# Another order of the three interleaved chains in a layer's mixer

## The chip, the cores and the metric

The kernel runs on one core of one Trainium2 chip. The metric is the device time of one execution in microseconds (us), lower is better. The engines are TensorE (PE, its weight loads shown as PEld), VectorE (DVE), ScalarE (ACT), GpSimd (POOL), and SyncE (SP), which here issues the transfers.

## The reference, cut to what matters

The network is a first block (window attention, a state space mixer, a delta rule mixer, a feed-forward part) and then two layers. The change touches only the mixer of the first of these layers, the "even mixer", on 512 tokens:

```python
h = x @ w_in                       # q_a, c_kv, q_idx, k_idx, w_idx, q_b, k_b, v_b, f_in
q_lat = einsum('bshd,hrd->bshr', q_a, w_uk) * HEAD_DIM ** -0.5
log_f = log_sigmoid(f_in + b_f); cum_f = cumsum(log_f, axis=1)
# for each block of 128 queries:
idx = einsum('bthd,bsd->bths', qi, k_idx)
score = einsum('bth,bths->bts', wi, relu(idx))      # masked to be causal
_, sel = top_k(score, k_sel)                        # 128 keys of each query
la = ql @ c_sel + bias[t5_bucket];  oa = softmax(la) @ c_sel      # 8 latent heads
lb = qb @ k_b + cum_f - cum_f_keys; ob = softmax(lb) @ v_b        # 8 forget heads
out = concat([oa @ w_uv, ob]) @ w_o
```

## The kernel before

All matrix products with large weights are made of three passes of float32r halves (helper `three`, L570 to L572): high by high, high by low, low by high. The weights come in a list of chunks; ACT makes the high half of a chunk (L1260), DVE or, for chunks 52 to 63, POOL the low half (L2450).

In the even mixer each engine runs the same three generators, and `walk` steps them in the order of one string of 444 letters, `even_order()`. A letter is a step of a chain, and each engine meets its own part of that step at this place of its in-order queue:

- **F** (156 steps), `dense_even`: the projection, chunks 53 to 62. A step is the three passes of one of 8 slices of k into a bank of 512 columns (chunk 56, the second half of the values, takes 12 products of 256 columns in a step). The last four steps turn the output of the forget heads (`otb`) for the output product.
- **I** (96 steps), `index`: three steps for small work (the decay sums among it), then for each of three query blocks 8 score steps (PE L1019 `ps<-kiT,qiT`, ACT relu into `rel` L1617, DVE sum into `sco` L2233) and 16 top-k steps on DVE alone; at last 8 heads of latent queries (`ql`, L1030) and position bias (`near`, L1036), with four steps for the values `va` (L1044).
- **A** (192 steps), `units`: 64 attention units, one for each head and query block, in three stages with lag: scores (L1054, L1058), turning the probabilities (L1076), and the product with the values (L1091, `ota` or `otb`).

All index products of PE go through one bank, number 7: the next one waits until ACT has emptied it. ACT's relu in turn waits until DVE has summed the relu two heads back, since `rel` has two buffers:

```python
clear(7)
w.wait_ge(*even.act.at("ki"))
e.matmul(ps[7][:, 0:n], qiT[...], kiT[s, 0:n], ...).then_inc(*idx.pe.one("s", i, h))
bank[7] = [idx.act.at("relu", i, h)]
```

`kiT` is what ACT copies out of the second bank of chunk 55 (L1575), and the product of chunk 55 with all its slices stands ahead of it. The engines' code of the stage stands in `dense_even`, `index` and `units` of each engine's program, called by `walk(EVEN_ORDER, ...)` at L1097, L1664, L2292, L2586 and L2720. The first and the odd mixer have orders of their own.

Of the kernel before, what the change touches and what calls it, by code (L numbers as in the profile page):

```python
# [246 lines left out]


def even_order():
    return ("FFFFFIFFFFFFFFFFFFFFFFFFFFFIFFFFFFFFFFFFFFFFIFFFFFFFIFIFFIFIFIFIFIFIFFFIFFIIFFIIIIFFFFIIFFFFIFIIFAFIFFFIIIFFIFFIAFAFFAIA"  # L250
            "AAAIAAFAIAAIAFAFIAIFFIAIFAAAAFFAAIAAFIAAIFAAIAAIAIFAIFAAAFAIFIFAIFFFFIIAAIAIAFFIAFAFAAIFFAAIAAIAFFAIFFIAFIAFAIAAFAFIAFAI"
            "AFAIAIIAAFAAIFIFFAIAAFFIAAAFFFFFAAFFIAIAAAFIAAFIAIFFIFAAIAAAFIIAAFAFIAFAAAAIAAIAFIAAIFAIAAFIAAAAAIAAAAAIAAAFAAAAIAAAAAFI"
            "AFAAFAIAAAAIAAAAAAAFAFIAAAAFAIAAAAAIAAAAIAAAAAAAAAAIAAAAAAAAAAIAAAAAAAFAAAAFAAAFAAFA")


def odd_order():
# [5 lines left out]
def build(nc, ins, out):  # L262
    plan = weight_plan()
    offs = [0]
    for c in plan:
        offs.append(offs[-1] + 128 * chunk_width(c))
    u_dram = nc.dram_tensor("u_scratch", (8, 384), F32, kind="Internal").ap()
    IN_ORDER, EVEN_ORDER, ODD_ORDER = first_order(), even_order(), odd_order()

    ctx = ExitStack()  # L270
# [2597 lines left out]
```

## Time and profile before

| | before |
|---|---|
| median of 3 runs | 1930.08 us (1929.76 to 1931.78) |
| profiled execution, its own time | 1931.88 us |
| span of the profiled execution | 1930.0 us |
| PE busy | 1877.8 us (97%) |
| DVE, ACT, POOL busy | 978.8, 731.5, 249.5 us |
| mean granted clock of TensorE | 0.987 |

The even mixer's walk takes from 721 to 964 us of the span. A row of a timeline gives the start in us from the start of the span, the duration, the engine, the source line, the operation, what it writes and reads, the count, and, in brackets, the idle time of the engine before it and what ended it. A matmul's duration overlaps the next one, so the pace of PE is read from the distance of two starts.

### The profile page before, as it was taken

To read this page: it belongs to the slowest core of one execution; us is meant where nothing else is said; L and a number is where in the kernel's file an instruction comes from. 1 tells how busy PE (TensorE), PEld (TensorE's weight loads), DVE (VectorE), ACT (ScalarE), POOL (GpSimd) and SP (SyncE) were. 2 spreads that over 40 slices of the span, in tenths; PEclk is the share of its full clock that TensorE was granted. 3 is DMA by queue.
4 is the path that set the end of the run, shared out by engine and by line. 5 is a ranking of instruction groups with operands and counts; after the bars stand their busy time and mean duration, and the time that the engine had idled before them with its cause. 6 is when DMAs were issued, how large, how long until landed. Compare 5 with 4: busy or idle time off the path is not lost.

```text
span 1930.0 us, 23339 instructions
## 1 busy us (share of the span) xinstructions
PE 1877.8 (97%) x9766; PEld 1548.4 (80%) x9766; DVE 978.8 (51%) x1557; ACT 731.5 (38%) x1229; POOL 249.5 (13%) x168
## 2 busy tenths in 40 slices
PE   7999978999999999999999999999999999999998
PEld 6888967888888888767789888888778888888886
DVE  5676455323222254776566555522664475555334
ACT  6664444323231243556724434421333244434211
POOL 1433500111110023211000111100000001111000
PEclk9999979999999999999999999999999999999999
DMA  5211022132323232101022232232322313222321
GB/s 197 87 37 64 29 89 88 66 109 88 109 88 109 76 132 95 66 23 45 14 78 103 92 108 89 94 135 76 109 88 87 110 66 109 92 105 87 120 98 66
DMA packets 28764, 170.01 MB, mean 88 GB/s; under 512 B 3386, under 2 KB 5602, under 8 KB 10866
## 3 DMA queue, kind: packets, MB, share of 16 engines
q1 hardware_dynamic: 28660, 168.53, 25.4%
q8 instruction: 77, 1.26, 0.3%
q14 instruction: 27, 0.22, 0.0%
HBM read 166.37 MB, written 2.11 MB: 87 GB/s over the span
## 4 chain that ended last, share of the span: by engine, by line
PE 90%; DVE 8%; ACT 1%; issue 1%; DMA 0%; POOL 0%; SPq 0%; DVEq 0%; ACTq 0%
PE ps L570 26%; PE ps L572 26%; PE ps L571 26%; PE ps L1091 2%; DVE wL L1781 1%; PE ps L1019 1%; PE ps L1054 1%; PE ps L1058 1%; PE ps L1076 1%; DVE x L2316 1%; DVE x L2311 1%; DVE hL L1788 1%; PE ps L685 1%; PE ps L650 1%; PE ps L849 0%
## 5 line engine op out<-in xcount | busy, mean ns | idle before, releaser
L570 PE MATMUL ps<-hH,wH 128*128 128x512 f32 (+1 forms) x1568 | 604.2, 385 | 7.8 <-DVE hL L1788 4.8
L571 PE MATMUL ps<-hL,wH 128*128 128x512 f32 (+1 forms) x1568 | 592.0, 378 | 0.0
L572 PE MATMUL ps<-hH,wL 128*128 128x512 f32 (+1 forms) x1568 | 592.0, 378 | 0.0
L1781 DVE TENSOR_TENSOR wL<-raw,wH 128x1024 fp32r<-128x1024 f32 (+2 forms) x250 | 306.2, 1265 | 378.2 <-ACT wH L1260 378.2
L1260 ACT ACTIVATE wH<-raw 128x1024 fp32r<-128x1024 f32 (+2 forms) x298 | 290.5, 1024 | 281.8 <-PE ps L572 281.8
L570 PEld LDWEIGHTS ps<-hH,wH 128*128 128x128 f32 x1568 | 297.2, 190 | 69.1 <-issue 5.9
L572 PEld LDWEIGHTS ps<-hH,wL 128*128 128x128 f32 x1568 | 296.8, 189 | 54.2
L571 PEld LDWEIGHTS ps<-hL,wH 128*128 128x128 f32 x1568 | 297.2, 190 | 52.6 <-issue 1.4
L570 PE MATMUL ps<-wH,aH 128*128 128x512 f32 x528 | 209.0, 396 | 0.0
L571 PE MATMUL ps<-wL,aH 128*128 128x512 f32 x528 | 208.8, 395 | 0.0
L572 PE MATMUL ps<-wH,aL 128*128 128x512 f32 x528 | 208.8, 395 | 0.0
L2336 DVE SCALAR_TENSOR_TENSOR ft<-ps,cols,ft 128x511 f32<-128x511 f32 (+1 forms) x176 | 131.4, 746 | 133.1 <-ACT ft L1689 130.0
L2450 POOL TENSOR_TENSOR wL<-raw,wH 128x1024 fp32r<-128x1024 f32 (+3 forms) x48 | 111.9, 2351 | 341.9 <-ACT wH L1260 341.9
L2549 POOL TENSOR_TENSOR aL<-ft,aH 128x512 fp32r<-128x512 f32 x44 | 57.1, 1297 | 683.7 <-ACT aH L1695 683.7
L570 PE MATMUL ps<-wH,hH 128*128 128x512 f32 (+2 forms) x320 | 115.6, 361 | 3.6 <-DVE wL L1781 3.6
L572 PEld LDWEIGHTS ps<-wH,aL 128*128 128x128 f32 x528 | 99.3, 188 | 24.0
L570 PEld LDWEIGHTS ps<-wH,aH 128*128 128x128 f32 x528 | 99.3, 188 | 23.8
L571 PEld LDWEIGHTS ps<-wL,aH 128*128 128x128 f32 x528 | 99.3, 188 | 23.8
L572 PE MATMUL ps<-wH,hL 128*128 128x512 f32 (+2 forms) x320 | 111.7, 349 | 0.0
L571 PE MATMUL ps<-wL,hH 128*128 128x512 f32 (+2 forms) x320 | 111.7, 349 | 0.0
L1689 ACT ACTIVATE ft<-ps,cols 128x512 f32<-128x512 f32 x88 | 59.9, 681 | 72.0 <-PE ps L572 72.0
L2160 DVE TENSOR_TENSOR ft<-ft,ps 128x512 f32<-128x512 f32 x22 | 15.1, 687 | 120.4 <-PE ps L572 120.4
(370 smaller groups left out, 1907.9 us busy)
## 6 DMA issues: line engine op xcount, KB each, us to landing
raw<-in_wbig SPq DMA_DIRECT2D x139, 1024.0 KB, 4.9
rows<-in_rows SPq DMA_DIRECT2D x12, 512.0 KB, 5.9
x<-in_x SPq DMA_DIRECT2D x8, 512.0 KB, 5.4
raw<-in_wbig SPq DMA_DIRECT2D x8, 512.0 KB, 3.5
out<-x SPq DMA_DIRECT2D x4, 512.0 KB, 2.6
near<-u_scratch SPq DMA_DIRECT2D x1, 1024.0 KB, 6.9
raw<-in_wbig SPq DMA_DIRECT2D x1, 1000.0 KB, 7.5
raw<-in_wbig SPq DMA_DIRECT2D x1, 600.0 KB, 10.2
```

The lines of the kernel that those rows point to most:

```text
L570: e.matmul(o, hi, m_hi, start=first, stop=False)
L571: e.matmul(o, hi, m_lo, start=False, stop=False)
L572: return e.matmul(o, lo, m_hi, start=False, stop=end)
L650: m = e.transpose(ps[b][:, 128 * k:128 * k + 128], src[:, o:o + 128], ident[:, :])
L685: m = e.matmul(ps[b][:, 128 * j:128 * j + 128], v3(da)[:, i, h:h + 1].broadcast_to([128, 128]), U[:, :], start=True, stop=True)
L1091: t = e.matmul(ps[6][:, 0:64], Pt[n % 2][:, 128 * j:128 * j + 128], v[:, j, 64 * h:64 * h + 64], start=j == 0, stop=j == i)
L1260: e.activation(wH[r][:, cs], raw[r][:, cs], ACT.Copy).then_inc(*cast.one(c, h))
L1689: e.activation(ft[s][:, :], ps[b0 + t][:, :], ACT.Identity, scale=cols[:, column + 2:column + 3]).then_inc(*ffn.act.one("y", c, t))
L1781: e.tensor_tensor(wL[r][:, cs], raw[r][:, cs], wH[r][:, cs].bitcast(F32), ALU.subtract).then_inc(*low_dve.one(c, h))
L2336: e.scalar_tensor_tensor(y[:, d:512], ps[b0 + t][:, 0:512 - d], cols[:, column + 2 - d:column + 3 - d], y[:, d:512], ALU.mult, ALU.add).th ...
L2450: e.tensor_tensor(wL[r][:, cs], raw[r][:, cs], wH[r][:, cs].bitcast(F32), ALU.subtract).then_inc(*low_pool.one(c, h))
L2549: e.tensor_tensor(aL[:, m, :], ft[t0 + m % 2][:, :], aH[:, m, :].bitcast(F32), ALU.subtract).then_inc(*ffn.pool.one("lo", c))
```

## The change

The string that `even_order()` returns is replaced by another with the same 156 F, 96 I and 192 A. Each chain keeps its own order; only how they are interleaved changes, on all five engines at once. Nothing else changes: same operations, tiles, banks and waits.

```diff
 def even_order():
-    return ("FFFFFIFFFFFFFFFFFFFFFFFFFFFIFFFFFFFFFFFFFFFFIFFFFFFFIFIFFIFIFIFIFIFIFFFIFFIIFFIIIIFFFFIIFFFFIFIIFAFIFFFIIIFFIFFIAFAFFAIA"
+    return ("FFFFFIFFFFFFFFFIFFFFIFFFFFFFFFFFFFFFFFFFFFFFFFFFFFFIFIFIIIIFIFIIFFFIIFFFFFIFIFFIIIFIIFIFFFFFFIFFFIAIFFIAIIFAIFFAIAFIAAAI"
...
-            "AFAAFAIAAAAIAAAAAAAFAFIAAAAFAIAAAAAIAAAAIAAAAAAAAAAIAAAAAAAAAAIAAAAAAAFAAAAFAAAFAAFA")
+            "FIAAAAAIAAAIAAAAAAAAIAAAIAAAAAAAAAIAAAIAAAAAAAAAAIAAAIAAAAAAAAFAAAAAAAAAAAAFAAAFAAFA")
```

Counted over the string, the maximal groups of F steps with another product of PE on each side are 61 before and 54 now. The last F step that is not one of the four turns is letter 388 before and letter 361 now, of 444; the first of the four turns is letter 431 before and 423 now.

**PE, the first index score.** `wH_51`, `wL_53` with `hH_56`, `hL_57` as the second operand are chunk 56 (256 columns), `hH_56<-wH_52` 512 columns wide is chunk 55, `kiT_181,qiT_177` is the first score product. Before:

```order
L572 MATMUL ps<-wH_51,hL_57 128x256
L570 MATMUL ps<-wH_51,hH_56 128x256
L571 MATMUL ps<-wL_53,hH_56 128x256
L572 MATMUL ps<-wH_51,hL_57 128x256
L1019 MATMUL ps<-kiT_181,qiT_177 128x256
```

Now:

```order
L570 MATMUL ps<-hH_56,wH_52 128x512
L571 MATMUL ps<-hL_57,wH_52 128x512
L572 MATMUL ps<-hH_56,wL_54 128x512
L1019 MATMUL ps<-kiT_181,qiT_177 128x256
L570 MATMUL ps<-wH_51,hH_56 128x256
```

The first step of chunk 56 (12 products) stood between chunk 55 and the score; now the score follows chunk 55 directly.

**PE, the third to the sixth score of the first query block.** Before, there was a step of chunk 56 (12 products) behind each of them, as here around the third:

```order
L571 MATMUL ps<-wL_53,hH_56 128x256
L572 MATMUL ps<-wH_51,hL_57 128x256
L1019 MATMUL ps<-kiT_181,qiT_178 128x256
L570 MATMUL ps<-wH_51,hH_56 128x256
L571 MATMUL ps<-wL_53,hH_56 128x256
```

Now:

```order
L572 MATMUL ps<-wH_51,hL_57 128x256
L1019 MATMUL ps<-kiT_181,qiT_178 128x256 x2
L1019 MATMUL ps<-kiT_181,qiT_179 128x256 x2
L570 MATMUL ps<-wH_51,hH_56 128x256
```

The four follow each other with nothing between them.

**ACT, from the copy of `kiT` on.** `wH_52<-raw_50` are the two casts of chunk 57, `rel` the relus of the scores, `vb` the copies out of the banks of chunk 56:

```order
 L1575 ACTIVATE ckvT_174<-ps 128x512
 L1575 ACTIVATE kiT_181<-ps 128x512
-L1260 ACTIVATE wH_52<-raw_50 128x1024 x2
 L1617 ACTIVATE rel_202<-ps 128x256
-L1560 ACTIVATE vb_188<-ps 128x256
+L1260 ACTIVATE wH_52<-raw_50 128x1024 x2
 L1617 ACTIVATE rel_203<-ps 128x256
 L1560 ACTIVATE vb_188<-ps 128x256
 L1617 ACTIVATE rel_202<-ps 128x256
 L1617 ACTIVATE rel_203<-ps 128x256
-L1560 ACTIVATE vb_188<-ps 128x256
 L1617 ACTIVATE rel_202<-ps 128x256
```

The first relu now stands ahead of the two casts, the second directly behind them. On SP the two transfers of the decay sums (L2713, L2714) move ahead of one chunk's load; on POOL nothing moves.

## Rows read from the trace of the kernel before

**Rows 1.** The page: PE's busy time, and the chain that ended last

```profile
PE 1877.8 (97%) x9766; PEld 1548.4 (80%) x9766; DVE 978.8 (51%) x1557; ACT 731.5 (38%) x1229; POOL 249.5 (13%) x168
...
PE 90%; DVE 8%; ACT 1%; issue 1%; DMA 0%; POOL 0%; SPq 0%; DVEq 0%; ACTq 0%
```

**Rows 2.** Windows: the walk's stretch, by engine; last PEclk, DMA share, GB/s

```profile
721.00:966.00 245.00, 244.34 (x1253) 182.94 (x1254) 155.19 (x486) 135.38 (x345) 50.06 (x24) 1.00 0.16 52
```

**Rows 3.** Waits of PE, 728 to 966 us (total us, times, longest)

```profile
PE ps L1091 <- ACT ota L1660: 0.4, 1, 0.4
```

**Rows 4.** Timeline of PE around the first index scores

```profile
754.44 0.39 PE L572 MATMUL ps<-hH,wL 128*128 128x512 f32 x1
754.67 0.28 PE L570 MATMUL ps<-wH,hH 128*128 128x256 f32 x1
...
755.98 0.28 PE L572 MATMUL ps<-wH,hL 128*128 128x256 f32 x1
756.19 0.70 PE L1019 MATMUL ps<-kiT,qiT 64*128 64x256 f32 x2
756.82 0.39 PE L570 MATMUL ps<-wH,hH 128*128 128x256 f32 x1
...
758.44 0.70 PE L1019 MATMUL ps<-kiT,qiT 64*128 64x256 f32 x2
```

**Rows 5.** Timeline of ACT, the same stretch

```profile
754.87 0.60 ACT L1575 ACTIVATE kiT<-ps 128x512 f32<-128x512 f32 x1 [4.84 <-PE ps L572]
755.36 2.00 ACT L1260 ACTIVATE wH<-raw 128x1024 fp32r<-128x1024 f32 x2
757.26 0.37 ACT L1617 ACTIVATE rel<-ps 128x256 f32<-128x256 f32 x1
...
759.17 0.39 ACT L1617 ACTIVATE rel<-ps 128x256 f32<-128x256 f32 x1 [0.24 <-PE ps L1019]
```

**Rows 6.** Timeline of DVE: the sums of the scores

```profile
757.66 1.49 DVE L2233 SCALAR_TENSOR_TENSOR sco<-rel,widx,CM 128x256 f32<-128x256 f32 x1 [13.97 <-ACT rel L1617]
759.60 2.10 DVE L2233 SCALAR_TENSOR_TENSOR sco<-rel,widx,sco 128x256 f32<-128x256 f32 x1 [0.44 <-ACT rel L1617]
763.29 0.48 DVE L2233 SCALAR_TENSOR_TENSOR sco<-rel,widx,sco 128x256 f32<-128x256 f32 x1 [1.59 <-ACT rel L1617]
```

**Rows 7.** Timeline of POOL, the same stretch

```profile
756.49 4.92 POOL L2450 TENSOR_TENSOR wL<-raw,wH 128x1024 fp32r<-128x1024 f32 x2 [6.13 <-ACT wH L1260]
```

**Rows 8.** Timelines of PE, then ACT: a latent query product and its copy

```profile
902.76 1.12 PE L1030 MATMUL ps<-qaT,wuk 64*128 64x512 f32 x2
903.82 0.44 PE L1076 MATMUL ps<-ident,rows 128*128 128x128 f32 x2
...
903.92 0.60 ACT L1625 ACTIVATE ql<-ps 128x512 f32<-128x512 f32 x1 [1.31 <-PE ps L1030]
```

**Rows 9.** Timelines of PE, then ACT: the end of the walk

```profile
960.48 0.66 PE L1091 MATMUL ps<-va,Pt 128*128 128x64 f32 x4 [0.39 <-ACT ota L1660]
...
959.62 0.60 ACT L1268 ACTIVATE hH<-ps 128x512 fp32r<-128x512 f32 x1
960.12 0.31 ACT L1660 ACTIVATE ota<-ps,sx 128x64 f32<-128x64 f32 x1
```

**Rows 10.** Timeline of PE: a group of F steps between other work

```profile
875.70 0.48 PE L570 MATMUL ps<-hH,wH 128*128 128x512 f32 x1
876.02 0.39 PE L571 MATMUL ps<-hL,wH 128*128 128x512 f32 x1
876.25 0.40 PE L572 MATMUL ps<-hH,wL 128*128 128x512 f32 x1
```

**Rows 11.** Timelines of DVE, then SP: the decay sums and their transfer

```profile
743.28 0.41 DVE L2225 TENSOR_SCALAR cf<-cf 8x512 f32<-8x512 f32 x1
...
750.76 0.78 SPq L2713 DMA_DIRECT2D QB<-cf  x1
```

**Rows 12.** Waits of PE's weight loads, 728 to 966 us: first and last of 12 rows with a named releaser

```profile
PEld ps L1091 <- ACT rows L1644: 2.5, 4, 0.8
...
PEld ps L1030 <- DVE mb L2257: 0.2, 1, 0.2
```

**Rows 13.** Windows of another stage of the kernel, where PE had stood idle

```profile
250.00:253.00 3.00, 0.00 (x0) 0.00 (x0) 2.38 (x4) 2.14 (x9) 0.03 (x1) 0.98 0.00 0
253.00:258.00 5.00, 0.65 (x9) 0.53 (x9) 1.26 (x5) 3.85 (x12) 0.00 (x0) 0.50 0.00 0
258.00:263.00 5.00, 5.00 (x26) 5.00 (x24) 2.83 (x9) 1.15 (x3) 0.00 (x0) 0.50 0.01 2
```

More of the change, by code:

```diff
@@ L249, in even_order @@
 def even_order():
-    return ("FFFFFIFFFFFFFFFFFFFFFFFFFFFIFFFFFFFFFFFFFFFFIFFFFFFFIFIFFIFIFIFIFIFIFFFIFFIIFFIIIIFFFFIIFFFFIFIIFAFIFFFIIIFFIFFIAFAFFAIA"
-            "AAAIAAFAIAAIAFAFIAIFFIAIFAAAAFFAAIAAFIAAIFAAIAAIAIFAIFAAAFAIFIFAIFFFFIIAAIAIAFFIAFAFAAIFFAAIAAIAFFAIFFIAFIAFAIAAFAFIAFAI"
-            "AFAIAIIAAFAAIFIFFAIAAFFIAAAFFFFFAAFFIAIAAAFIAAFIAIFFIFAAIAAAFIIAAFAFIAFAAAAIAAIAFIAAIFAIAAFIAAAAAIAAAAAIAAAFAAAAIAAAAAFI"
-            "AFAAFAIAAAAIAAAAAAAFAFIAAAAFAIAAAAAIAAAAIAAAAAAAAAAIAAAAAAAAAAIAAAAAAAFAAAAFAAAFAAFA")
+    return ("FFFFFIFFFFFFFFFIFFFFIFFFFFFFFFFFFFFFFFFFFFFFFFFFFFFIFIFIIIIFIFIIFFFIIFFFFFIFIFFIIIFIIFIFFFFFFIFFFIAIFFIAIIFAIFFAIAFIAAAI"
+            "AFIAAAIAAIAFAIAFFFFIAFAIFFFIAIAFFFAIAFAFAIFIAAIAAAFFIFAFAAAIAFFIAIAAIAFIAAIIFAFFAIAFFFAFIAAFFIAAIAAAIAIAAAIAIAAIAFFFAIAF"
+            "FAFFIFIAFAFAFFFFIAFAFIAIFAAFIFAFAAFFIAAIAIAAIFAFFIAIFFAFFAIAFAFAFIIFAAAIFFFAAFAAAAIAAIAIAAIAAIFAIAAAAAAIAAAAAIAAAFAAAAIA"
+            "FIAAAAAIAAAIAAAAAAAAIAAAIAAAAAAAAAIAAAIAAAAAAAAAAIAAAIAAAAAAAAFAAAAAAAAAAAAFAAAFAAFA")
 def odd_order():
```

## Prediction

> **What bounds the kernel now.** I read the page first: TensorE is busy for 97% of the span and carries 90% of the chain that ended last [rows 1]. Then the windows, for the stretch in which the changed order rules: of 245.00 us from 721 to 966 PE is busy for 244.34, at a granted clock of 1.00, that is 2.4 GHz, while DVE has 155, ACT 135 and POOL 50 us [rows 2]. Then PE's waits: from 728 us to the end of the walk one single wait shows, 0.4 us behind ACT's copy of `ota` [rows 3]. So the stage is bound by the issue of PE, and an order can win only what lies between the products, while any order that sends PE to a bank too early loses that time one for one, since no later slack on PE can take it up. A busy PE is not PE at its peak, so below I go by distances of starts, not by durations.
>
> **The change, step by step.** All terms are PE time in the walk.
>
> *1. The first score comes without cover.* The last product of chunk 55 starts at 754.44 and the next step at 754.67; ACT's copy to `kiT` starts at 754.87 and takes 0.60, so `kiT` is ready at 755.47 [rows 4, 5]. Before, PE had the first step of chunk 56 meanwhile (754.67 to 756.19) and asked for `kiT` only then. Now the score is the next thing and PE stands still from 754.67 to 755.47: **+0.80 us**. Queued behind it on PE is everything of the walk. The two casts that stood on ACT ahead of the first relu now stand behind it. They move about 1.3 us later and POOL's low half with them, but chunk 57 is used only after chunk 56, whose eight steps take about 12 us (756.19 less 754.67 is 1.52 each), against 4.92 us for POOL's two passes [rows 4, 7]: no cost. If that cover were gone, the 1.3 us would be paid.
>
> *2. Four scores in a row.* A score product's start to its relu's start is 759.17 less 758.44, 0.73 us, and the relu takes 0.39 [rows 4, 5]; the next score can't start before 1.12 us have passed, while the product itself takes PE only 0.63 (756.19 to 756.82). That is 0.49 us of idle time at each of three junctions, **+1.5 us**. Before, 1.5 us of chunk 56 stood in each. The relu in turn needs the DVE sum two heads back. Where POOL was at work the sum took 1.49 and 2.10 us, where it was not, 0.48; POOL's two passes lie exactly there [rows 6, 7]. If the second pass again holds a sum, the fifth score's relu waits some tenths for it: I take **+0.2**. The bounds are nothing (the sum done in 0.48) and one whole pass, 4.92 / 2 = 2.5 us.
>
> The Trainium skill has a rule for it: on its page "SBUF — State Buffer", section "SBUF: two separate sides", the port pair that VectorE and GpSimd share is an exclusive lock held for a whole instruction, and a VectorE instruction with two SBUF inputs has to wait for it. The rows of 1.49 and 2.10 us agree with it; by the rule the delay here ends with POOL's pass, so it speaks for the upper bound of 2.5 us more than for 0.2, and the sum would then be 2.3 us higher.
>
> *3. The other bank 7 junctions.* The widest are the latent queries: product's start to ACT's start 903.92 less 902.76, 1.16 us, and 0.60 for the copy, so 1.76 between two users of the bank, of which the product fills 1.06 [rows 8]. So 0.70 us of other work must stand behind each. Adding up the products that the new order puts there, I get 0.76 us at the tightest two of the eight, 0.89 and more at the others; in the second and third block of scores the tightest gaps hold about 0.65 us, enough for the narrower relu and some 0.1 short for the wide one. **+0.1 us.** At the end of the walk the 0.4 us of before comes from ACT doing the turned half `hH` (0.60 us) ahead of the copy of `ota` (0.31) [rows 3, 9]. The last letters are unchanged, so it stays; but the first of the four turns has moved eight letters forward, where the next user of that bank stands only about half a microsecond behind. The same collision there costs between 0 and 0.4: **+0.2 us.**
>
> *4. Fewer groups of F.* The first product of a group takes 0.32 us to the next start (875.70 to 876.02) where the second takes 0.23 [rows 10]. With 61 groups reduced to 54, 7 times 0.09: **-0.6 us**. Ends: 0, if that is paid by whatever follows, and -1.3, if leaving a group costs as much as entering it.
>
> *5. What is moved at no cost.* SP: the transfers of the decay sums are now ahead of one load, and SP waits at them until DVE has made the sums. That is at 743.28 + 0.41 = 743.69, and the transfer went out only at 750.76 [rows 11], behind that load, which waits for POOL's low half two chunks back. So SP is through its new wait before the load could have gone anyway, and the sums land earlier. If the sums were 7 us later, the load would be late by what is over. DVE: the top-k steps (16 for each block) are spread over more of PE's time than before, which makes the attention maxima queue less; since PE did not wait for them, this gives nothing. The last F steps are now 27 letters earlier, about 13 us of PE's work, so the last attention units have only each other as cover; they had that before too for the last 56 letters, without a wait other than the one at the end.
>
> Sum: 0.8 + 1.5 + 0.2 + 0.1 + 0.2 - 0.6 = **+2.2 us**. The span of the profiled execution would go from 1930.0 to 1932.2, and its own time from 1931.88 to 1934.1. It was slower than the median of the runs shown by 1.8 us, so the median goes from 1930.08 to 1932.3.
>
> **The rivals.** A measurement of this kernel can tell about 0.2%, 3.9 us, from no change: that is 1926.2 to 1933.9.
>
> - *POOL's pass holds the sums in the burst* (slower). Place: the fourth to sixth score. It decides when the sum of the third score starts while POOL's second pass runs, which is likely, and the pass has over 2 us to go, which is less likely: the relu of the first score is now ahead of the casts, which shifts POOL later, towards the burst. Price: 2.5 in place of 0.2, sum +4.5, **1934.6**. Chance 0.12.
> - *The end without filler* (slower). With the last F steps gone from the 20 or so units ahead of the end, each `ota` junction could pay what the weight loads show. Twelve rows of their waits have a named releaser, 25 times and 11.8 us together, the first 2.5 us in 4 times [rows 12]; 0.15 us on each of 20 units is 3 us, and with the sum **1935.3**. Against it: PE paid next to nothing for them before, with the same units at the same pace. Chance 0.09.
> - *The clock falls* (slower). In another stage PE stood idle around 250 to 253 us and worked at 0.50 of the clock, 1.2 GHz, afterwards, for at least 253 to 263 [rows 13]. In the burst PE is idle for about 2.5 of 12 us. If the clock fell for 10 us of wall time, PE would do 5 us less: **1937.3**. Chance 0.04. The Trainium skill names that danger on its page "TensorE: Matmul & The Clock Gate", section "A second HAM failure mode: psum-queue depth-cycling": small idle times between groups, each waiting for a bank, can make the clock swing. No row of this stage shows it.
> - *The looser spacing pays* (faster). PE's ends are modelled, so a part of the 11.8 us of late weight loads [rows 12] may be real time although only 0.4 us shows as idle. If half of it were and went away, -5.9 on top of +2.2 gives -3.7 and, with the other end of term 4, -4.4: **1925.7**. For it: top-k and maxima are less crowded on DVE. Against it: the starts of PE around those places are at their ordinary distances of 0.23 us [rows 10]. Chance 0.10.
>
> **How the numbers follow.** The likeliest case, the sum with its small terms, has chance 0.65; its own range is from +0.3 (terms 2 and 3 at their low ends, 4 at its far end) to +3.9. The range of all is 1928.5 to 1935.8: it holds the first two rivals and some of the fast one's partial forms, and leaves out the clock and the full fast case. Faster by over 0.2%: 0.10; within 0.2%: 0.65; slower: 0.12 + 0.09 + 0.04 = 0.25.
>
> **What would show it.** In the profile after: a wait of PE or its weight load for ACT's `kiT` of about 0.8 us at about 754.7; three distances of about 1.1 us between score starts directly behind each other, where the product takes 0.63; a sum on DVE of over 1 us in that stretch; the end of the walk some 2 us later, and the rest of the span only shifted. If PE's starts in the burst are 0.63 us apart, term 2 is wrong. If the stage up to 754 us or between 770 and 950 changes its length by more than 1 us either way, what I left out of the sum was not nothing. A clock under 1.00 between 755 and 770 would be the third rival.

## The result and the profile after

| | before | changed |
|---|---|---|
| median | 1930.99 us (1929.76 to 1932.47, 8 runs) | 1939.29 us (1934.34 to 1939.75, 8 runs) |
| profiled execution, its span | 1930.0 us | 1937.6 us |
| mean granted clock of that execution | 0.987 | 0.986 |

The changed kernel is slower. Its median is 8.3 us higher where 2.2 were forecast; the ratio over all executions is 1.0035, 95% interval 1.0025 to 1.0046, which is 6.8 us, since two of the eight lie lower than the rest. Its executions form two groups: two at 1934.34 and 1934.70 us with a mean granted clock of 0.988, and six from 1938.23 to 1939.75 us with 0.985 to 0.986. The mean clock of an execution is a blunt gauge: in the profile before, the clock is at 0.50 for about 49 us, all of them outside the walk, and in the one after for about 55 us, of which 13.7 lie in the walk.

The page after, busy times and the chain, against [rows 1]:

```profile
PE 1882.7 (97%) x9766; PEld 1552.8 (80%) x9766; DVE 976.7 (50%) x1557; ACT 730.8 (38%) x1229; POOL 249.3 (13%) x168
...
PE 90%; DVE 7%; ACT 1%; issue 1%; DMA 0%; POOL 0%; SPq 0%; DVEq 0%; ACTq 0%
```

PE is busy for 4.9 us more with the same 9766 products. That is the first sign that idle time is not the whole story, since it would not make the products themselves take longer.

The waits of PE after, 728 to 975 us (in total, times, longest), against [rows 3]:

```profile
PE ps L1019 <- ACT rel L1617: 1.4, 3, 0.5
PE ps L1019 <- ACT kiT L1575: 0.8, 1, 0.8
PE ps L1091 <- ACT ota L1660: 0.4, 1, 0.4
```

Two new rows, 2.2 us together, are the forecast terms 1 and 2. The timeline of PE after shows the place, against [rows 4]; the last column is the idle time ahead of the row:

```profile
754.86 0.39 PE L572 MATMUL ps<-hH,wL 128*128 128x512 f32 x1
756.03 0.67 PE L1019 MATMUL ps<-kiT,qiT 64*128 64x256 f32 x2 [0.78 <-ACT kiT L1575]
...
757.08 0.28 PE L570 MATMUL ps<-wH,hH 128*128 128x256 f32 x1
757.19 0.28 PE L571 MATMUL ps<-wL,hH 128*128 128x256 f32 x1
...
760.49 0.70 PE L1019 MATMUL ps<-kiT,qiT 64*128 64x256 f32 x2
761.66 0.70 PE L1019 MATMUL ps<-kiT,qiT 64*128 64x256 f32 x2 [0.47 <-ACT rel L1617]
762.83 0.70 PE L1019 MATMUL ps<-kiT,qiT 64*128 64x256 f32 x2 [0.47 <-ACT rel L1617]
764.00 1.22 PE L1019 MATMUL ps<-kiT,qiT 64*128 64x256 f32 x2 [0.47 <-ACT rel L1617]
765.14 0.58 PE L570 MATMUL ps<-wH,hH 128*128 128x256 f32 x1
765.52 0.41 PE L571 MATMUL ps<-wL,hH 128*128 128x256 f32 x1
765.73 0.41 PE L572 MATMUL ps<-wH,hL 128*128 128x256 f32 x1
765.95 0.41 PE L570 MATMUL ps<-wH,hH 128*128 128x256 f32 x1
```

Read the distances of starts. The scores of the burst are 1.17 us apart. The last of them lasts 1.22 us instead of 0.70, and behind it the products of chunk 56 start 0.21 us apart (765.52, 765.73, 765.95), where they had been 0.11 to 0.12 apart (757.08, 757.19). The windows of after give the granted clock (the column behind POOL), against [rows 2]:

```profile
754.00:763.50 9.50, 7.78 (x40) 5.15 (x38) 3.65 (x4) 4.37 (x8) 4.86 (x2) 1.00 0.11 42
763.50:777.20 13.70, 13.23 (x50) 10.81 (x50) 5.10 (x15) 1.92 (x5) 0.00 (x0) 0.50 0.22 78
777.20:975.00 197.80, 197.22 (x1025) 145.19 (x1025) 129.54 (x455) 117.25 (x317) 30.11 (x16) 1.00 0.11 38
```

For 13.7 us, from just ahead of the burst's last score (764.00) on, the clock was 0.50, that is 1.2 GHz; ahead and behind, 1.00. Before the fall PE had been busy for 7.78 of 9.50 us: the idle time of 1.72 us is the wait for `kiT` and the first two of the burst. The third wait lies at the fall itself.

DVE's sums and POOL's low halves after, against [rows 6, 7]:

```profile
757.15 0.48 DVE L2233 SCALAR_TENSOR_TENSOR sco<-rel,widx,CM 128x256 f32<-128x256 f32 x1 [13.04 <-ACT rel L1617]
759.39 1.41 DVE L2233 SCALAR_TENSOR_TENSOR sco<-rel,widx,sco 128x256 f32<-128x256 f32 x1 [1.75 <-ACT rel L1617]
761.64 2.83 DVE L2233 SCALAR_TENSOR_TENSOR sco<-rel,widx,sco 128x256 f32<-128x256 f32 x3 [0.84 <-ACT rel L1617]
...
758.14 4.86 POOL L2450 TENSOR_TENSOR wL<-raw,wH 128x1024 fp32r<-128x1024 f32 x2 [7.36 <-ACT wH L1260]
```

The two sums that overlap POOL's passes (758.14 to 763.00) are long again: 1.41 us, and 1.64 us for the first of the three in the last row of DVE. That one ended at 763.28, and the relu two heads later started at 763.56, 0.28 us behind. So no score came later for it, but the margin was narrow.

To compare versions I take the **walk**: from the start of its first own product on PE (L1007) to the start of the last L1091. It is 238.97 us before and 247.38 after, +8.41 us; what follows it takes 966.1 and 964.9.

### The profile page after: what moved, and what is told of

It is laid out like the page before. It is cut to its first block, busy times and chain, and to the rows that moved or that the text cites. A ratio compares the mean times of both kernels' runs of the same rounds, so it can differ in the third digit from the quotient of the medians.

```text
span 1937.6 us, 23339 instructions
## 1 busy us (share of the span) xinstructions
PE 1882.7 (97%) x9766; PEld 1552.8 (80%) x9766; DVE 976.7 (50%) x1557; ACT 730.8 (38%) x1229; POOL 249.3 (13%) x168
## 4 chain that ended last, share of the span: by engine, by line
PE 90%; DVE 7%; ACT 1%; issue 1%; DMA 0%; POOL 0%; SPq 0%; DVEq 0%; ACTq 0%
PE ps L570 26%; PE ps L572 26%; PE ps L571 26%; PE ps L1091 2%; PE ps L1019 1%; DVE wL L1781 1%; PE ps L1054 1%; PE ps L1058 1%; PE ps L1076 1%; DVE x L2316 1%; DVE x L2311 1%; DVE hL L1788 1%; PE ps L685 1%; PE ps L650 1%; PE ps L849 0%
```

## The experiments

Two theories stood first. **A**: the idle time in chunk 56's scores brings the clock down, and the low clock costs more than the idle time. **B**: the fall belongs to something else in the new order (what follows, its transfers, its spacing), and the idle time only costs its 2.2 us. The letters shown are those around chunk 56's first score, of one line of the string.

**The burst taken apart.** a_spread leaves the first score uncovered; a_cover covers it and keeps the burst; a_clean does both.

```diff
-FFFIFIFIIIIFIFIIFFFIIF    changed order
+FFFIFIFIFIFIFIFIFIFIII    a_spread
+FFFFIFIFIIIIFIFIIFFIIF    a_cover
+FFFFIFIFIFIFIFIFIFIIII    a_clean
```

> The new order, but with one step of chunk 56 behind each of the eight scores of the first query block (the 19 letters from the first score on are eight times IF and then III). The first score still follows chunk 55 directly. Theory A (the burst's idle time brings the clock down, and the fall costs more than the idle time itself): the three idle times of 0.47 us go, 0.8 us for kiT stays, the granted clock is 1.00 from 755 to 780 us in every execution, times in one group at about 1931 us, within 1 us of the kernel before. Theory B (something else of the new order costs 5 us, for example the lack of F steps near the end or the order around it, and the clock is only seen with it): most times stay at 1938 to 1940.

> The new order, but with the first step of chunk 56 ahead of the first score, so that kiT is ready; the four scores in a row stay. Theory A with the burst alone as cause: 0.8 us of idle time goes, the clock still falls in many executions: two groups of times, near 1932.5 and near 1938. If the sum of all idle time decides (2.2 us), 1.4 us may be too little for the fall, and all times lie at 1932 to 1933. Theory B: 1938 to 1939, all but unchanged.

> The new order with both repairs: a step of chunk 56 ahead of each of the eight scores. Theory A: no idle time in this stretch and no fall of the clock; the time is what the rest of the new order gives, by the sum of the prediction -0.6 + 0.3, so 1930 to 1931 us, with the kernel before inside the interval. Theory B: 1937 or more.

**The burst kept, its waits taken away.** a_bank puts the scores of the odd heads into a second bank, 6, so that a product need not wait for the relu just ahead of it:

```diff
-clear(7)
+clear(bk := 6 if i == 1 and h % 2 else 7)
-e.matmul(ps[7][:, 0:n], qiT..., kiT[s, 0:n], ...)
+e.matmul(ps[bk][:, 0:n], qiT..., kiT[s, 0:n], ...)
-bank[7] = [idx.act.at("relu", i, h)]
+bank[bk] = [idx.act.at("relu", i, h)]
```

> The new order to the letter, but the odd heads' scores of the first query block go to bank 6 (unused until the attention units begin) instead of bank 7, so that a score needs not wait for the relu just before it. 0.8 us for kiT stays, the three waits of 0.47 us should go. Theory A: no fall of the clock, 1931 us. A third theory, that the clock falls for what is issued there (eight narrow products of 64 rows and 96 of 256 columns in a row, no wait needed), gives the fall again and 1937 us or more.

**The idle time filled with useless work.** a_pad computes more than the reference asks for: a product with the identity whose result nobody reads, ahead of the fourth to sixth score.

```diff
+if i == 1 and h in (3, 4, 5):
+    clear(6)
+    e.matmul(ps[6][:, 0:256], ident[:, :], qiT[0][:, 0:256], start=True, stop=True)
 clear(7)
```

> The new order with one product of a 256-column stretch with the identity, into bank 6 and read by nobody, ahead of the fourth, fifth and sixth score of the first query block (work added, output unchanged). It takes PE 0.43 us where PE would wait 0.47 us for the relu. Theory A (PE's idleness brings the clock down, not the late scores as such): the waits' time stays, their idleness goes: clock 1.00, 1932 to 1933 us. If it is the narrow products and not the idleness: 1938 to 1939, as without them.

| | median, us (runs) | ratio to before, 95% | walk in its profile | PE's waits at chunk 56 | clock 0.50 |
|---|---|---|---|---|---|
| changed | 1939.29 (8) | 1.0035 [1.0025, 1.0046] | 247.38 | 0.8 and 1.4 | 13.7 us |
| a_spread | 1932.58 (11) | 1.0011 [1.0002, 1.0021] | 240.59 | 0.8 | none |
| a_cover | 1934.55 (11) | 1.0023 [1.0015, 1.0032] | 245.08 | 1.4 | 10.2 us |
| a_clean | 1932.30 (11) | 1.0011 [1.0002, 1.0019] | 239.75 | none | none |
| a_bank | 1930.90 (11) | 1.0003 [0.9994, 1.0012] | 239.57 | 0.8 and 0.5 | none |
| a_pad | 1933.70 (11) | 1.0016 [1.0007, 1.0024] | 241.88 | 0.8 | none |

The fall goes with the waits of the burst: the two versions with all three of them (changed, a_cover) have it, the four without do not. Some expectations missed in size. a_spread and a_clean lie 2.1 and 1.8 us above before, not within 1, and their intervals leave 1 out; a_clean's walk is 0.8 us longer than that of before without a wait of its own. a_cover gave no two groups but a spread from 1932.24 to 1936.86 us. a_pad lies 0.7 us above its range.

a_bank does more than take waits away. Its timeline of PE:

```profile
760.23 0.70 PE L1019 MATMUL ps<-kiT,qiT 64*128 64x256 f32 x4
761.40 0.97 PE L1019 MATMUL ps<-kiT,qiT 64*128 64x256 f32 x4 [0.47 <-ACT rel L1617]
762.30 0.38 PE L570 MATMUL ps<-wH,hH 128*128 128x256 f32 x1
```

A score is two products, so x4 is two scores, and the third and fourth together take 0.70 us, as long as one score in the changed kernel. Even and odd heads use different halves of the 128 rows (the slice `s`), and with two banks neither waits for the other; whether it is the halves that let them run side by side was not tested. The four scores occupy PE for 2.07 us, one idle time included. With one bank at full clock they take 4.13 us (b_both below, 763.59 to 767.72). So the good time of a_bank, and of a_best and b_best below, is in part this gain and not only the waits.

a_pad is the plainest of them. Its timeline of PE (the added lines shift L1019 to L1022, and L1019 is the filler):

```profile
760.09 0.70 PE L1022 MATMUL ps<-kiT,qiT 64*128 64x256 f32 x2
760.72 0.70 PE L1019 MATMUL ps<-qiT,ident 128*128 128x256 f32 x2
761.34 0.70 PE L1022 MATMUL ps<-kiT,qiT 64*128 64x256 f32 x2
761.97 0.70 PE L1019 MATMUL ps<-qiT,ident 128*128 128x256 f32 x2
762.60 0.70 PE L1022 MATMUL ps<-kiT,qiT 64*128 64x256 f32 x2
```

and its windows:

```profile
754.00:763.50 9.50, 8.72 (x43) 5.69 (x42) 4.04 (x4) 4.54 (x9) 4.87 (x2) 1.00 0.06 22
763.50:777.20 13.70, 13.70 (x91) 11.70 (x91) 8.62 (x26) 4.29 (x9) 0.74 (x1) 1.00 0.24 79
```

The scores are still 1.25 us apart, as slow as with the waits (1.17), and the order, the transfers and DVE's work are those of the changed kernel. Only the idle time is gone, and with it the fall: 91 products in 763.5 to 777.2 us where the changed kernel had 50, and a walk shorter by 5.50 us although more is computed. The median is 5.6 us lower (1939.29 less 1933.70), or 5.1 when each is taken against the runs of before made beside it (1930.99 and 1930.47 us). That is A, and against B.

**Is it this place?** a_late is a_bank with a burst at the second query block's scores (one bank, 384 columns) instead:

```diff
-AIFFIAIIFAIFFAIAFIAAAIA    a_bank
+AIFFIAIIIIIFAFFAAFAAAIA    a_late
```

> The new order with the two banks for the first block's scores (no waits there), and the first four scores of the second query block (384 columns) put in a row. Idle by the rows of before: start to relu 0.95 and 0.49 for it, less 0.84 for the product, 0.6 us at each of three junctions, and more at the third if DVE is still at its top-k steps. If any such burst brings the clock down, the fall shows at about 790 us and the median is 1936 to 1938; if the stretch of chunk 56, whose products are narrow, is part of the cause, the clock stays at 1.00 and the median is 1932.5 to 1934.

It gave 1936.14 us (9 runs), ratio 1.0027 [1.0017, 1.0037]. Its waits and windows (of the 2.3 us, 0.5 belong to the first block's scores and 1.8 to the new burst):

```profile
PE ps L1019 <- ACT rel L1617: 2.3, 4, 0.6
...
780.00:791.80 11.80, 10.01 (x39) 6.43 (x37) 10.10 (x31) 3.96 (x6) 4.68 (x2) 1.00 0.30 99
791.80:798.60 6.80, 6.80 (x16) 4.55 (x15) 1.54 (x6) 3.04 (x7) 0.00 (x0) 0.51 0.28 119
```

Again the clock falls at the end of the burst, 28 us later in the program and for 6.8 us; the profile is that of its fastest execution, 1933.91 us. The effect belongs to the burst, not to chunk 56.

**The old order with the same burst.** If A were all, the burst put alone into the order of before would lose the clock too. b_burst covers the first score, b_both does not:

```diff
-FFFFIFIFFIFIFIFIFIFIF    order of before
+FFFIFFIFFIIIIFFFFIFIF    b_both
+FFFFIFIFFIIIIFFFFIFIF    b_burst
```

> The order of before, with two things of the new one: the first score ahead of the first step of chunk 56, and the third to sixth score in a row (18 letters from IF on: IFFIFFIIIIFFFFIFIF; the other 426 letters are those of before). Theory A (these two waits and the fall of the clock that follows them are the whole loss): idle 0.8 + 3 x 0.47 us, clock 0.50 for some 10 us from about 763 us in most executions, median 1937 to 1939.5. Theory B (other parts of the new order take a share of the 8 us): 1932 to 1934.

> The order of before with the third to sixth score in a row alone (FIFIFFIIIIFFFFIFIF), the first score covered as before. Theory A, by what the new order gave with the first score covered: some executions with the clock at 0.50 for 10 us and some without or with a shorter one, median 1933 to 1936, wider scatter than before. If the fall needed the wait for kiT too: 1931.5 to 1932.5.

b_both had exactly the waits of the changed kernel (0.8 and 1.4 us) and **no fall** in its profile, and none shows in the clock or the time of its 11 executions (all at 0.989): 1932.26 us, ratio 1.0009 [1.0000, 1.0018]. That is outside theory A's range of 1937 to 1939.5. In b_burst the clock fell for 3.4 us and the median is 1933.84, 1.0017 [1.0008, 1.0026]; its profile is of an execution of 1931.99 us, and its slower ones, up to 1935.02 us with a mean clock of 0.987, were not profiled. So A as first put was too simple: the same idle time can be had with or without the fall. What differs between b_both and the changed kernel, in these letters, is that two F steps instead of one stand ahead of the second score and ahead of the burst, and that four F steps instead of F and score by turns stand behind it. Four more versions make a square of the two:

```diff
 order of before, burst early (IFIFIIII) or late (IFFIFFIIII), and then turns or F steps
+FFFIFIFIIIIFIFIFFFFFF    b_same: early, turns behind it
+FFFIFIFIIIIFFFFIFIFFF    c_earlyrun: early, four F steps behind it
+FFFIFFIFFIIIIFIFIFFFF    c_lateturn: late, turns behind it
 changed order, four F steps behind the burst
+FFFIFIFIIIIFFFFIFIFIII   a_follow
```

> The order of before everywhere, except that the eighteen instructions from chunk 56's first score on stand as in the changed order: F and score by turns, then scores 3 to 6 in a row, then F and score by turns again. Theory (where the burst lies and what follows it decide whether and how long the clock is low): the same waits as in the changed kernel (kiT 0.8 us once, rel 0.47 us three times) and the same two-by-two stretch behind them, so the granted clock falls to 0.50 for 10 us or more in most executions, and the median is 1937 to 1939.5. Rival (the fall needs another part of the new order too): no fall, the median 1932 to 1934, that is before plus the 2.2 us of idle.

> The changed order with the four scores in a row kept where they are, but the four F steps that stood between and behind the last scores directly behind the burst, and the scores left over after them. Theory (what follows the burst decides how long the clock stays low): the waits stay (kiT 0.8, rel 3 times 0.47 us), the clock may still fall, but for 3 to 7 us and not for 13.7; median 1933.5 to 1936. Rival (the burst alone decides the length): 0.50 for 13.7 us again and 1938 to 1939.5.

> The order of before, with the burst of four scores one more pair of F steps later (as where no fall was seen), but F and score by turns behind it as in the changed order. Theory 1 (what follows the burst decides whether the clock falls): a fall of 7 us or more in most executions, median 1935 to 1939. Theory 2 (what stands ahead of the burst decides whether it falls): no fall in most executions, median 1932 to 1933.5.

> The order of before, with the burst at the changed order's place (score, F, score, F, four scores) and four F steps behind it. Theory 1 (what follows decides whether): no fall or one of 3 to 4 us, median 1932 to 1933.5. Theory 2 (what stands ahead decides whether, what follows decides how long): a fall of about 7 us, 2.9 us of PE's time, median 1934.5 to 1936.5.

| same waits, 0.8 and 1.4 us | turns behind the burst | four F steps behind it |
|---|---|---|
| burst early, order of before | b_same: 1937.30 (5 runs), clock low for 10.2 us, walk 245.27 | c_earlyrun: 1935.86 (6), 6.8 us, 243.65 |
| burst early, changed order | changed: 1939.29 (8), 13.7 us, 247.38 | a_follow: 1936.07 (6), 6.8 us, 244.47 |
| burst late, order of before | c_lateturn: 1932.89 (11), none, 240.81 | b_both: 1932.26 (11), none, 240.84 |

The ratios to before are 1.0032 [1.0019, 1.0044] for b_same, 1.0030 [1.0018, 1.0042] for c_earlyrun, 1.0029 [1.0017, 1.0040] for a_follow and 1.0015 [1.0007, 1.0024] for c_lateturn. Of c_lateturn's 11 executions ten lie at 1931.19 to 1933.09 us and one at 1938.70 with the lower clock. The windows of c_earlyrun, then of c_lateturn:

```profile
754.00:770.00 16.00, 13.80 (x65) 10.51 (x64) 5.09 (x6) 5.09 (x10) 4.87 (x2) 0.80 0.27 95
770.00:790.00 20.00, 20.00 (x109) 16.98 (x109) 9.86 (x31) 5.49 (x10) 4.76 (x2) 0.99 0.15 54
```

```profile
754.00:770.00 16.00, 13.80 (x82) 10.36 (x81) 4.76 (x6) 5.73 (x12) 4.74 (x2) 1.00 0.24 90
770.00:790.00 20.00, 20.00 (x106) 16.97 (x106) 12.57 (x38) 6.36 (x10) 7.07 (x3) 1.00 0.16 54
```

PE's busy time is the same 13.80 of 16 us in both, and the clock 0.80 in one and 1.00 in the other. So in this square **where** the burst lies goes with whether the clock falls: early, it did in all four profiles and, by times and clocks, in most executions; late, in one of 22 by its time and clock. **What follows** goes with how long it stays low, by one profile of each version (b_same's is its slowest execution; two of its five took 1933.83 and 1934.26 us): 6.8 us with four F steps behind the burst in both orders, 10.2 and 13.7 us with turns. In the early versions the kiT wait ends at 756.03 and the first wait of the burst at 761.66, 5.6 us later; late, in b_both:

```profile
756.25 0.67 PE L1019 MATMUL ps<-kiT,qiT 64*128 64x256 f32 x2 [0.78 <-ACT kiT L1575]
...
764.76 0.70 PE L1019 MATMUL ps<-kiT,qiT 64*128 64x256 f32 x2 [0.47 <-ACT rel L1617]
```

8.5 us lie between. That the two idle places act together when close would fit, and a_cover, which has the burst alone, did fall less than the changed kernel. But b_burst has its burst late too (two F steps ahead of it), less idle time than b_both, and did fall. So neither the place nor the sum of the idle time decides alone; something else, perhaps the moment at which the burst comes, plays a part that no run here separates. This stays open.

**Is the rest of the new order good?** a_best and b_best take away what the burst cost (an F step ahead of the first score, and the second bank) in the changed order and in that of before:

```diff
+FFFFIFIFIIIIFIFIIFFIIF    a_best (changed order, two banks)
+FFFFIFIFFIIIIFFFFIFIF     b_best (order of before, two banks)
```

> The changed order with an F step ahead of the first score (which covers the wait for kiT) and the odd heads' scores in a second bank (which takes away the waits for rel). Both theories: no idle time in chunk 56's scores, the clock stays at 0.99; it tells what the rest of the new order costs: 1930 to 1931 us, 0 to 0.5 above before. If the rest of the new order costs as much as the alternating version lost, 1932.

> The order of before with four scores in a row behind three F steps, and the second bank: no wait for kiT, none for rel, fewer changes between the kinds of products. Expected 1929.5 to 1930.5, that is 0 to 1 us below before, which is below or at what can be told; if the second bank itself costs (a product more to clear it), 1931.

a_best: 1930.44 us, ratio 1.0000 [0.9991, 1.0009], walk 238.79. b_best: 1929.43 us, 0.9996 [0.9987, 1.0004], walk 237.98. Neither can be told from before. With the same burst, cover and banks the new order's walk is 0.8 us longer than the old one's, in one profile of each. Apart from the second bank, a_best is a_cover (1934.55 us) and b_best is b_burst (1933.84): the bank alone took away the fall and some 4 us in both orders. In both, PE's waits are the same, one in the burst (a score that waits for the relu two heads back in its bank) and the old one at the end:

```profile
PE ps L1019 <- ACT rel L1617: 0.5, 1, 0.5
PE ps L1091 <- ACT ota L1660: 0.4, 1, 0.4
```

## Why the prediction was wrong, step by step

The forecast said slower by 2.2 us, within 0.2%; the medians are 8.3 us apart, and 1939.29 lies above the range. The sum, as the runs put it (times of the walk):

| term | forecast | measured |
|---|---|---|
| 1 `kiT` without cover | +0.80 | +0.78 |
| 2 four scores in a row | +1.5, and +0.2 for DVE and POOL | +1.41 (3 times 0.47), and 0 |
| 3 other bank 7 junctions, first turn | +0.1, +0.2 | no wait of PE there |
| 4 fewer groups of F | -0.6 | in the burst -0.3; rest of the order, with 3, about +0.8 |
| clock | 0 (rival, chance 0.04) | +5.7 |
| sum | +2.2 | +8.4 |

The -0.3 is b_both's walk less that of before (240.84 less 238.97, 1.87) less its idle time (0.78 and three times 0.47, 2.19). The +0.8 is a_best less b_best, 238.79 less 237.98. By distances of starts, the way the forecast counted, each junction of term 2 is 0.54 (1.17 less 0.63), 1.62 in all, and the saving in the burst then -0.5. The +0.8 has a second witness without burst or second bank: a_clean's walk less that of before, 239.75 less 238.97. And 5.7 is what is then left of 8.41. Each is from one profile of a version, so tenths are not sure. The rows give the same price by another way: at the low clock the products of 256 columns are 0.21 us apart instead of 0.12, so 13.7 us hold 43% less work, 13.7 x 0.43 = 5.9 us. The other versions agree: a_follow has 6.9 us less of low clock than the changed kernel and a walk shorter by 2.9, 0.42 for each us. The Trainium skill, on its page "TensorE: Matmul & The Clock Gate", section "HAM oscillation — how this bites in real kernels", counts half of the throttled time as lost, which as an estimate is 6.8 us for 13.7 us. The rows and runs here say 5.7 to 5.9, and they decide.

*Step 1 and step 2* were right in place, cause and size, and their cover held: the casts moved later and PE waited for none of them. The *first rival*, POOL's pass holding the sums, did not occur. The sums were long as forecast, and both long ones end 0.28 us behind the end of a pass of POOL (760.80 behind 760.52, 763.28 behind 763.00). But the relus of the burst are 1.17 us apart, because each waits for its product and the product for the relu before, so the relu two heads later comes 2.34 us behind. When the third score's sum started, at 761.64, POOL's pass had 1.36 us to go and not the over 2 us that the rival wanted; 0.28 us were left. The mechanism shows once the bank is no longer the limit, on ACT in a_bank:

```profile
763.13 0.39 ACT L1617 ACTIVATE rel<-ps 128x256 f32<-128x256 f32 x1 [1.51 <-DVE sco L2233]
```

There a relu is held for 1.51 us of ACT's time by the sum. PE had the burst behind it by then and did not wait, so it cost nothing there either.

*Step 3*: none of its tight places shows as a wait of PE. The first of the four turns cost nothing visible, and the 0.4 us at the end stayed.

*Step 4* failed in size. A burst does save junctions (-0.3), but with that taken out the remaining order is 0.8 us worse, not better: 61 and 54 groups are no measure of it. PE's weight loads wait longer for DVE's `sx` now (L1054 and L1058 together 5.1 us, where the view of [rows 12] had 2.1; a_best has 5.1 and b_best 2.1 too), which may be a place of the 0.8; that was not tested. The *second rival*, the end without filler, did not come: the walk's last waits are as before.

*The range* was also added up wrongly: with terms 2 and 3 at their low ends and 4 at its far end the sum is 0.8 + 1.5 - 1.3, +1.0 and not +0.3. The result lies on the other side, so this decided nothing.

*The step that failed* is the clock: the sum put it at nothing, with a chance of 0.04 for the third rival, and it cost 5.7 us. The forecast wrote that in the burst PE is idle for about 2.5 of 12 us, worked out +5 us and 1937.3 from it, and gave it 0.04, because the only rows of a low clock in hand [rows 13] followed a stretch with no product at all. "No row of this stage shows it" was true of a stage that had next to no idle time to show (0.4 us), and was no evidence against it. The rule that the forecast cites there from the Trainium skill, page "TensorE: Matmul & The Clock Gate", section "A second HAM failure mode: psum-queue depth-cycling", describes the kind of thing that happened: small idle times between groups can make the clock swing, and the trace and the runs agree (0.50 from the end of the burst on, 1.00 in a_pad and a_bank). That rival's price was short too, 5 us where 5.7 to 5.9 were lost, since the low stretch was 13.7 and not 10 us. The waits themselves were forecast well (0.8 and 1.5 us, measured 0.78 and 1.41), but they are only a quarter of the loss. Why the clock falls in one place of the same burst and not in another stays open.

## What to carry to other kernels

Where PE is full, price a new idle place twice: what it lasts, and what the clock does behind it; here 2.2 us of waits brought on a further loss of 5.7 us. If products must follow each other through one bank, give them a second bank, or put other products (even useless ones: a_pad) between them; whether it also helps to keep other idle places away from them, these runs do not separate. This mends the new order, but it gains nothing on the old one: neither a_best nor b_best can be told from before. Judge a reordering by the versions that undo one run of letters, not by counts over the whole string.

## What was not expected of the hardware

- The granted clock fell to 0.50 with no idle time longer than 0.78 us: PE was busy for 7.78 of the 9.50 us ahead of the fall, with the clock at 1.00.
- The same four waits led to a low clock for 13.7, 10.2 and 6.8 us or to none, in versions that differ in what stands around them. By times and clocks one program also differs from execution to execution (1934.34 and 1939.75 us for the changed kernel, 1931.19 and 1938.70 for c_lateturn); one execution of each was profiled.
- A filler product of 256 columns in each gap kept the clock at 1.00 and made the kernel 5.1 to 5.6 us faster than leaving PE idle.
- With a second bank two scores of neighbouring heads, on different halves of the rows, took 0.70 us together, as long as one alone.
